# Feed-forward sums added straight from the banks and its loop written out, convolution taps dealt out, and a reordered second mixing layer

## The reference

```python
hn = rms_norm(h, g_mix_pre[i])
u = hn @ w_in[i]
q, k, v, xr, yg = jnp.split(u, [D_ATTN, 2 * D_ATTN, 3 * D_ATTN, 3 * D_ATTN + D_REC], axis=-1)
attn = neighborhood_attention(q, k, v, rpb[i])            # 8 heads of 128
rec = rglru_bidirectional(xr, conv_w[i], ...) * jax.nn.gelu(yg)   # 4-tap conv, two gates, two scans
mixed = jnp.concatenate([rms_norm(attn, g_attn_out[i]), rms_norm(rec, g_rec_out[i])], axis=-1) @ w_out[i]
h = h + rms_norm(mixed, g_mix_post[i])
fn = rms_norm(h, g_ffn_pre[i])
ff = (jax.nn.silu(fn @ w_ffn_gate[i]) * (fn @ w_ffn_up[i])) @ w_ffn_down[i]    # 5632 hidden
h = h + rms_norm(ff, g_ffn_post[i])
gate = jax.nn.sigmoid(rms_norm(h, g_ple_pre[i]) @ w_ple_gate[i])
h = h + rms_norm(gate * (p[i] @ w_ple_proj[i]), g_ple_post[i])
```

## Time and profile before

| | us |
|---|---|
| runs of the kernel | 4240.32, 4241.44, 4246.13 (median 4241.44) |
| the profiled execution | 4242.38 |
| its span in the profile | 4240.5 |
| PE busy | 4036.8 (95%) |
| DVE busy | 2759.2 (65%) |
| ACT busy | 1909.5 (45%) |
| POOL busy | 267.3 (6%) |
| mean granted share of PE's clock | 0.987 |

### The profile page before, as it was taken

One profiled execution on the slowest core, in us unless ns is written; L12 is line 12 of the kernel. 1 busy time (PEld: TensorE's weight loads), 2 busy tenths in 40 slices (PEclk: granted clock), 3 DMA queues, 4 the chain that ended last, 5 costly groups with the idle time before them and its releaser, 6 DMA issues.

```text
span 4240.5 us, 78225 instructions
## 1 busy us (share of the span) xinstructions
PE 4036.8 (95%) x30878; PEld 3846.5 (91%) x30878; DVE 2759.2 (65%) x3689; ACT 1909.5 (45%) x2772; POOL 267.3 (6%) x252
## 2 busy tenths in 40 slices
PE   2999999999999999999999999999888999999998
PEld 2999999999999999999999999999887888888888
DVE  7667777566678766677756576565466656565665
ACT  1443435334544344353533454454365544444465
POOL 0012121000000001212100000000000000000000
PEclk8999999999999999999999999999999999999999
DMA  9433333574358833333357434543443354555543
GB/s 392 154 130 118 132 115 128 206 272 154 140 191 315 298 136 123 120 133 119 130 192 278 160 138 149 182 176 133 168 146 114 137 189 179 179 179 185 179 143 120
DMA packets 114132, 724.38 MB, mean 171 GB/s; under 512 B 12608, under 2 KB 13056, under 8 KB 36224
## 3 DMA queue, kind: packets, MB, share of 16 engines
q1 hardware_dynamic: 88416, 639.17, 41.9%
q10 hardware_dynamic: 25504, 82.13, 5.4%
HBM read 719.09 MB, written 2.16 MB: 170 GB/s over the span
## 4 chain that ended last, share of the span: by engine, by line
PE 77%; DVE 8%; ACT 7%; issue 6%; DMA 1%; DVEq 0%; ACTq 0%; SPq 0%
PE bank L271 15%; PE bank L273 15%; PE bank L272 15%; PE bank L288 9%; PE bank L289 4%; ACT Wh L336 3%; PE bank L952 2%; PE bank L956 2%; PE bank L931 2%; DVE Wl L342 2%; DMA raw<-in_ada 1%; PE bank L2116 1%; PE bank L2118 1%; PE bank L2117 1%; PE bank L314 1%
## 5 line engine op out<-in xcount | busy, mean ns | idle before, releaser
L336 ACT CAST Wh<-raw 128x1024 fp32r<-128x1024 f32 x1140 | 1189.9, 1048 | 2020.8 <-PE bank L273 1509.8
L342 DVE TENSOR_TENSOR Wl<-raw,Wh 128x1024 fp32r<-128x1024 f32 x1140 | 1417.4, 1246 | 1002.0 <-ACT Wh L336 997.1
L271 PE MATMUL bank<-H,Wh 128*128 128x256 f32 x5536 | 1618.6, 292 | 0.5 <-ACT WS L1987 0.4
L272 PE MATMUL bank<-H,Wh 128*128 128x256 f32 x5536 | 1567.9, 283 | 0.0
L273 PE MATMUL bank<-H,Wl 128*128 128x256 f32 x5536 | 1567.2, 283 | 0.0
L271 PEld LDWEIGHTS bank<-H,Wh 128*128 128x128 f32 x5536 | 1063.0, 192 | 18.2 <-issue 17.4
L272 PEld LDWEIGHTS bank<-H,Wh 128*128 128x128 f32 x5536 | 1063.8, 192 | 9.2 <-issue 8.6
L273 PEld LDWEIGHTS bank<-H,Wl 128*128 128x128 f32 x5536 | 1062.2, 192 | 0.0
L288 PE MATMUL bank<-H,Wh 128*128 128x512 f32 x1600 | 561.9, 397 | 10.9 <-ACT WS L2170 5.6
L289 PE MATMUL bank<-H,Wl 128*128 128x256 f32 x1600 | 446.9, 279 | 0.0
L288 PEld LDWEIGHTS bank<-H,Wh 128*128 128x128 f32 x1600 | 300.3, 188 | 84.7 <-ACT WS L2170 6.2
(11 more groups left out here) (374 smaller groups left out, 4947.9 us busy)
## 6 DMA issues: line engine op xcount, KB each, us to landing
raw<-in_stream SPq DMA_DIRECT2D x572, 1024.0 KB, 4.8
WS<-in_ada ACTq DMA_DIRECT2D x94, 512.0 KB, 6.6
raw<-in_ada SPq DMA_DIRECT2D x32, 1024.0 KB, 7.5
gm_more<-in_ada ACTq DMA_DIRECT2D x20, 512.0 KB, 6.9
WS<-rows_d ACTq DMA_DIRECT2D x16, 512.0 KB, 4.8
KR<-in_ada ACTq DMA_DIRECT2D x14, 512.0 KB, 6.8
X<-in_x_t SPq DMA_DIRECT2D x1, 2048.0 KB, 17.4
WS<-in_rpb ACTq DMA_DIRECT2D x8, 256.0 KB, 2.9
```

What stands on the lines that cost most here:

```text
L271: pe.matmul(out[:, 0:T], wh, xh[:, kt, :], start=first, stop=False)
L272: pe.matmul(out[:, 0:T], wh, xl[:, kt, :], start=False, stop=False)
L336: act.copy(Wh[:, n % 4, :], raw[:, (sbk + 2) % 4, k * (D // 2):(k + 1) * (D // 2)]).then_inc(hi_ready, 1)
L342: dve.tensor_tensor(Wl[:, n % 4, :], raw[:, (sbk + 2) % 4, k * (D // 2):(k + 1) * (D // 2)], Wh[:, n % 4, :].bitcast(F32), ALU.subtract).t ...
```

## The change

It has two sets of edits.

The first: `dn` no longer copies its bank on ACT. DVE adds the bank to Y itself, ahead of its `dve_low` of the same half, and the three parts of `hidden` go behind the halves 0, 1 and 4. The feed-forward's loop of 5 rounds is a Python loop, so its instructions are written out. The delta rule's convolutions are dealt out, two taps behind each n from 2 to 13.

The second: neighborhood attention is one written-out run over 8 heads, whose ninth step projects the first three tiles of recurrence round 0 (so round 0 keeps tile 3 only); both groups of 7 spins go. The scores wait for k only, the transposes of v for v. The setup of the recurrence is split: DVE's part (`dve_rgset`) goes into the ninth step, ACT's table and functions behind round 0, `dve_lam` behind DVE's round 0. The eight attention squares get buffers of their own (`sq8`), follow tile 3 of round 0 on ACT, and are summed by PE behind tile 0 of round 1; the other sums move behind tile 3 of their round. In the chain, ACT's exponentials, tanh and table load go ahead of the casts of tile 2 and the square root between them; on DVE `gi` and its products go between the two subtractions of tile 2, and scans and `rec` ahead of those of tile 3. Eight spins are put behind the last sum.

```diff
-            def conv(m):
+            def conv(m, taps):
...
-                for t in range(4):
+                for t in taps:
...
-                if n in (4, 5, 7, 9, 11, 12):
-                    conv((4, 5, 7, 9, 11, 12).index(n))
+                if 2 <= n < 14:
+                    conv(n // 2 - 1, (0, 1) if n % 2 == 0 else (2, 3))
...
+        HN = D // 2 // P
-        def pe_na(pe, i):
+        def pe_na(pe):
...
-            for h in range(5):
+            for h in range(HN + 1):
                 x = (h - 1) % 2
                 if h:
-                    pe.wait_ge(tile_taken, i * 12 + (F2 + 3 * h + 2))
+                    pe.wait_ge(tile_taken, F2 + 3 * h - 1 + 2)
...
-                    if h < 4 and (h or n > 3):
+                    if h or n > 3:
...
                     if h and n == 1:
+                        pe.wait_ge(tile_taken, F2 + 3 * h + 2)
...
                     if h and n == 3:
-                        if h == 4:
-                            pe_spin(pe, 7)
...
+                        if h == HN and n == 1:
+                            S.wait(act, "pe", f"score{HN - 1}")
+                            st_rgset.wait(act, "dve", "z1")
...
+                        if h == HN:
+                            act.copy(rg_dst(b % 4), src).then_inc(tile_taken, 1)
...
+                        if h == HN:
+                            dve_rgset(dve)
...
+        def dve_lam(dve):
+            S = st_rgset
             S.wait(dve, "act", "ln")
             S.wait(dve, "dve", "pos")
             S.done(dve.tensor_tensor(lam4, lam4, SEC_X[:, 48:64], ALU.add), "dve", "softplus")
             S.wait(dve, "dve", "softplus")
             S.done(dve.tensor_scalar(lam4, lam4, -4.0, None, ALU.mult), "dve", "lam4")
+
+        def rg_dst(b):
+            return yin[:, b // 2, :] if b % 2 else xin[:, b // 2, 2:2 + T]
...
+        sq8 = [ws(4104 + j * T, T) for j in range(8)]
+
+        def rec_sq(j):
+            return sq8[j] if j < 8 else RSQ[:, j % 2, :]
...
             for b in range(4):
-                if gemm:
+                if gemm and (i or b == 3):
...
-                if i == 0:
-                    pe_rec_sum(pe, 2 * b)
-                    pe_rec_sum(pe, 2 * b + 1)
-                if i > 1 and b == 1:
-                    pe_rec_sum(pe, 2 * i + 4)
-                    pe_rec_sum(pe, 2 * i + 5)
+                if i == 1 and b == 0:
+                    for j in range(8):
+                        pe_rec_sum(pe, j)
...
+                if i > 1 and b == (3 if gemm else 1):
+                    pe_rec_sum(pe, 2 * i + 4)
+                    pe_rec_sum(pe, 2 * i + 5)
...
                 pe_rec_sum(pe, KT - 1)
+                pe_spin(pe, 8)
...
+                if chain and b == 2:
+                    S.wait(act, "dve", "log_a", r)
+                    S.done(act.activation(aa, ga_t, ACT.Exp), "act", "a")
+                    S.done(act.activation(hh, ga_t, ACT.Exp, scale=2.0), "act", "a2")
+                    S.wait(act, "act", "a2", r)
+                    S.done(act.activation(ga_t, ga_t, ACT.Tanh), "act", "tanh_la")
+                    act_table(act, ROOTS)
+                if gemm and (i or b == 3):
                     act_cast(act, i + Q_R, b, 0)
+                if chain and b == 2:
+                    S.wait(act, "dve", "expm1", r)
+                    S.done(act.activation(hh, hh, ACT.Sqrt, scale=-1.0), "act", "root")
+                if gemm and (i or b == 3):
                     act_cast(act, i + Q_R, b, 1)
...
+                if i == 0 and b == 3:
+                    for j in range(8):
+                        act_rec_square(act, j)
+                if i == 1 and b == 3:
+                    act_rstd(act, st_n[1], B[4][:, 0:T], 0, D // 2, "ra", "s7")
...
         def act_dn(act, q, f, run, par_, hidden):
-            S = st_dn
-            S.start("act")
             for b in range(4):
                 for k in range(2):
                     act_cast(act, q, b, k)
                     h = 2 * b + k
-                    if h < 2:
-                        S.wait_runs(act, "dve", run)
-                    else:
-                        S.wait(act, "dve", f"y{h - 2}", run)
-                    act.wait_ge(half_used, q * 8 + (h + 1))
-                    if h == 0:
-                        act.wait_ge(tile_taken, f + 2)
-                    act.copy(fd[k], G[k][:, :].rearrange("p (a b) -> p a b", b=T)).then_inc(tile_taken, 1)
...
         def dve_dn(dve, q, f, run, par_, hidden):
...
+                    h = 2 * b + k
+                    dve.wait_ge(half_used, q * 8 + (h + 1))
+                    dve.wait_ge(tile_taken, f + (h + 2))
+                    dve.tensor_tensor(Y[:, 2 * h:2 * h + 2, :], Y[:, 2 * h:2 * h + 2, :], G[k][:, :].rearrange("p (a b) -> p a b", b=T), ALU.add).then_inc(tile_taken, 1)
                     dve_low(dve, q, b, k)
-                    h = 2 * b + k
-                    dve.wait_ge(tile_taken, f + (h + 1 + 2))
-                    if h == 0:
-                        S.wait_runs(dve, "dve", run)
-                    S.done(dve.tensor_tensor(Y[:, 2 * h:2 * h + 2, :], Y[:, 2 * h:2 * h + 2, :], fd[k], ALU.add), "dve", f"y{h}")
+                    if hidden and h in (0, 1, 4):
+                        dve_hidden(dve, *hidden, parts=((0, 1, 4).index(h),))
...
-            with eng.Fori(0, (FF_GROUPS - 1) // 2) as i:
+            for i in range((FF_GROUPS - 1) // 2):
```

More of the change, by code:

```diff
@@ L1769, in pool_na, with dve_na @@
+        def pool_na(pool):
             S = st_na
             S.start("pool")
-            for h in range(4):
-                S.wait(pool, "dma", f"bias{h}", i)
+            for h in range(HN):
+                S.wait(pool, "dma", f"bias{h}")
                 v = bias[h % 2].rearrange("p a (r c) -> p (a r) c", c=64)
                 S.done(pool.tensor_tensor(v, v, const("near").unsqueeze(1).to_broadcast([P, 8, 64]), ALU.add), "pool", f"bias{h}")
-        def dve_na(dve, i):
+        def dve_na(dve):
@@ L1802, in dve_na @@
+                    if h < HN and n in (1, 4):
+                        at = 2 * h + n // 4
                         st_fin.wait(dve, "act", "r1")
@@ L1898, in pe_rec_sum @@
             S.wait(pe, "act", f"sq{j}")
-            S.done(pe.matmul(B[4][:, 0:T], ones, RSQ[:, j % 2, :], start=j in (0, 8), stop=j in (7, KT - 1)), "pe", f"s{j}")
+            S.done(pe.matmul(B[4][:, 0:T], ones, rec_sq(j), start=j in (0, 8), stop=j in (7, KT - 1)), "pe", f"s{j}")
         def pe_rg(pe, i, gemm, chain):
@@ L1965, in act_rg @@
                                                       bias=hb[:, bass.ds(r * 2 + (16 * x + 8 * z + m), 1)]), "act", f"gate{m}_{x}_{z}")
-                if chain and b == 2:
-                    S.wait(act, "dve", "log_a", r)
-                    S.done(act.activation(aa, ga_t, ACT.Exp), "act", "a")
-                    S.done(act.activation(hh, ga_t, ACT.Exp, scale=2.0), "act", "a2")
-                    S.wait(act, "act", "a2", r)
-                    S.done(act.activation(ga_t, ga_t, ACT.Tanh), "act", "tanh_la")
-                    act_table(act, ROOTS)
-                if chain and b == 3:
-                    S.wait(act, "dve", "expm1", r)
-                    S.done(act.activation(hh, hh, ACT.Sqrt, scale=-1.0), "act", "root")
-                if i == 0:
-                    act_rec_square(act, 2 * b)
-                    act_rec_square(act, 2 * b + 1)
                 if 1 < i < Q_RG and b == 0:
@@ L2011, in dve_rg @@
                     S.done(dve.tensor_tensor(gel, gel, yin, ALU.mult), "dve", "gel_arg")
-                if gemm:
+                if i == Q_RG and b == 2:
+                    for j in range(8):
+                        dve_lower(dve, st_n[1], mixed_w, j)
+                if chain and b == 2:
+                    S.wait(dve, "act", "tanh_la", r)
+                    S.done(dve.scalar_tensor_tensor(hh, hh, 1.0, ga_t, ALU.add, ALU.mult), "dve", "expm1")
+                if gemm and b == 2 and i:
+                    dve_low(dve, i + Q_R, b, 0)
+                if chain and b == 2:
+                    S.wait(dve, "act", "root", r)
+                    S.done(dve.scalar_tensor_tensor(gi_t, gi_t, 1.0, hh, ALU.add, ALU.mult), "dve", "gi")
+                    S.wait(dve, "dve", "gi", r)
+                    for m in range(2):
+                        S.done(dve.tensor_tensor(gi_t[:, 2 * m:2 * m + 2, :], gi_t[:, 2 * m:2 * m + 2, :], xc[:, m:m + 1, :].to_broadcast([P, 2, T]), ALU.mult), "dve", f"b{m}")
+                if gemm and b == 2 and i:
+                    dve_low(dve, i + Q_R, b, 1)
+                if chain and b == 3:
+                    for m in range(2):
+                        S.wait(dve, "dve", f"b{m}", r)
+                        S.done(dve.tensor_tensor_scan(hh[:, 2 * m, :], aa[:, 2 * m, :], gi_t[:, 2 * m, :], 0.0, ALU.mult, ALU.add), "dve", f"fwd{m}")
```

(9 more changed lines are left out.)

195 lines of the change are left out of this document (78 added, 117 removed).

## The result

The changed kernel takes 4180.27 us (median of four runs, 4177.27 to 4183.32), the kernel before beside it 4242.64. The ratio is 0.9848, with an interval from 0.9835 to 0.986: 62.4 us faster. The forecast was 4173, and 4180 lies in its range of 4161 to 4190; it lies 0.3 us outside the narrower 4165 to 4180, to which the prediction gave a chance of 0.71. Run once more beside another set of kernels, the changed kernel took 4185.39 against 4244.3, a ratio of 0.9855 (0.984 to 0.987), 58.9 us faster; single runs of it lie between 4177 and 4187, so a difference of 2 us between two kernels is small here.

The account below looks back on a forecast made before the run. PE was busy 95% of the span, so only its idle time, spins and half-speed stretches could be won. Terms summed to 68.7 us off 4242.4, giving 4173.7, and 4173 for the median; range 4161 to 4190.

Parts of the forecast that it names:

- Attention and round 0: Waits for the copy of v 13.8 us, two group ends 9.5, idle and slow time leaving round 0 12.4.
- Rounds 1 to 3: Recurrence: period 31.0 instead of 35.5 us, last chain starting at 99.7 instead of 109.1; 9.4 won, bounds 0 and 14.
- The feared wait for `Wl`: Recurrence rounds 2 and 3: line 271 waiting over 2 us for DVE's `Wl` would show the prediction wrong.
- Last pass: Recurrence's last pass, behind rounds 1 to 3: old order of ACT and DVE kept, so no gain forecast.
- Output projection's spins: Eight spins fill PE's 4.36 us idle ahead of line 310 and hold the clock: 2.7 us, bounds 0 and 3.4.
- Delta rule: Dealt-out taps remove line 911's 14 waits for DVE's subtraction: 4.1 us plus 0.2 for two first pairs, 4.3.
- Feed-forward: Loop pauses 8.1, entry 1.0, waits in `dn` 6.9 and end copy 0.6: 16.6 us, bounds 7 and 19.
- The additions: Feed-forward: DVE adding from the bank ends ten `dn` waits for ACT's copy, 6.9 us, and an end copy, 0.6.
- PE's pauses before line 288: Four later feed-forward rounds' starts: pauses read as the loop's jump, 8.1 us, gone when the loop is written out.
- the entry costs 1.0 more: Feed-forward loop's entry: 1.0 us more, taken as the loop's and gone with it.
- the prediction's own signs of being wrong: PE pauses in the written-out loop, a `Wl` wait over 2 us in rounds 2 and 3, or half clock there.
- Both rivals for a smaller gain: Recurrence gains nothing beyond round 0: 4185, chance 0.13; pauses at feed-forward rounds' starts not the loop's: 4182, chance 0.06.

Follow-up runs that it names:

- the second set's trace: The kernel before with the second set of edits alone, its feed-forward and loop unchanged: 4197.51 us against 4245.01, ratio 0.989.

## Why the prediction was right, and where it was not

- **Attention and round 0** (13.8 + 9.5 + 12.4 = 35.7): 35.9 in the trace. Waits priced with the modelled end and the slower first matmul (0.26 more than the table's idle time) came out right: from one head's scores to the next it takes 19.66 us instead of 21.40, 1.74 a head, where 13.8 for eight heads is 1.73.
- **Rounds 1 to 3** (9.4): 11.4. The period is 30.5, not 31.0, and the first convolution comes 6.3 behind round 0, not 6.7. The feared wait for `Wl` is there once, 1.6 us, not more, and the clock stayed up.
- **Last pass** (0): -2.9. "Behind that the last pass has the old order" was true of the order, not of the clock. The ple products behind the gates start 13.95 us behind the convolution in both kernels (3201.61 and 3144.69), and from there to the projection's first matmul of line 310 it takes 9.73 us instead of 6.82: the whole 2.9 is the products' half clock. In the kernel before the half clock had fallen on the gates' matmuls, ahead of that. The spins in the two pauses gave back 2.8 in the trace.
- **Output projection's spins** (2.7): 2.7, and 2.4 to 3.8 by the run without them.
- **Delta rule** (4.3): 7.4. The mechanism was right, the size was not: I left out the slower first matmul here, though I counted it at all other waits (0.29 + 0.10 + 0.04 for each wait instead of 0.29); layer 2 has another 0.08 a pair, and the two first pairs are worth 0.7, not 0.2.
- **Feed-forward** (16.6): 7.7. This is where the missing 9 us are, and it was two faults: the loop's price, and the interleaved start that came with it. The additions (6.9 for `dn`, 0.6 at the end) were right: `dn` 0.67 shorter ten times, and the end's wait 2.26 down to 0.46, 1.8 instead of 0.6. The failed step is "PE's pauses before line 288 ... with 0.16 + 0.1 each 8.1", "the entry costs 1.0 more", "both go with the loop". The pauses were the loop's and went; by the trace of the loop alone the feed-forward is 1.5 us shorter, not 9.1 (3.7 shorter than in the second set's trace, where the same old feed-forward takes 778.3; the medians give 3.2, and cannot tell it from nothing). Given back are the faster `gu` behind three edges (2.3, in part chance, as the second set's trace shows) and 0.22 in each of ten `dn` (2.2); a half-clock stretch in group 0, which the profile of before lacks and those of the changed kernel have too, takes 1.4; and the entry's 1.0 was never the loop's, since the step of 1.15 from matmul to matmul there is 1.12 without it. That leaves 0.7 of the 9.1 unassigned. The second fault: I read the loop's line and not what depends on its variable's type. The interleaved start in ten more groups took 4 to 7 us. Beside the additions the written-out `dn` is 0.79 shorter ten times (24.32 to 23.53), 1.0 more than forecast, so 16.6 - 7.6 + 1.2 + 1.0 - 3.9 = 7.3 of the 7.7 measured.
- The two edits of the feed-forward are not a sum of two terms. With the additions alone it takes 788.7 us, 12.6 more than before: the four jumps 1.9 more each, the `gu` behind them 11.2 more together (half clock, and the fast rhythm lost), a half clock of 1.4 in group 0, against 6.7 in `dn` and 1.8 at the end. With both, and group 0 alone interleaved, it takes 764.6. So writing the loop out was worth 1.5 by itself and 24 beside the additions, which alone would have been a loss. These are single traces, and the one of the additions alone is the slowest of its ten runs: by the medians that kernel loses 6.5 us, not 12, so 24 is a high figure.
- The rule of the Trainium skill (Runtime: NRT & Kernel Launch, section Instruction fetch mechanics), that a taken branch outside the fetched window stalls until the code is there, agrees with the packets: 16 KB of instructions 1.0 to 3.4 us behind the branch at the four taken edges of this loop, whose round has 1876 instructions in PE's records, and no such stop at the taken edges of the attention's and the delta rule's loops (1380 and 1210 instructions), where the branch lasts 0.2 us and PE has no pause. What the stall costs it does not say; here it was 2.1 and 3.9 us of PE.

Of the prediction's own signs of being wrong, one came in part: PE has pauses in the written-out feed-forward, 9.9 us idle of 732 where it forecast 0.14 us before each second half. Two are 2.4 us long, one in group 0, where the kernel before has it too, and one at the loop's entry, ahead of group 1's interleaved start. Of the 9.9, 9.3 are put down to VectorE's line 329, and none lies where the four jumps were. The other two did not come: the one wait for `Wl` is 1.6 us, below its 2, and rounds 1 to 3 ran at full clock.

Both rivals for a smaller gain fell by their own tests: the recurrence did gain beyond round 0, and the written-out code has no pause at the four later rounds' starts. The time of 4182 that the second of them gave came out all the same, by another mechanism. So the range held, and the 7 us between forecast and median are what is left of larger errors that cancel in part: +3.1 in the delta rule and +2.0 in rounds 1 to 3 stand against -2.9 in the last pass and -8.9 in the feed-forward, and the rest is within what one execution differs from the next.

## What to carry to other kernels

Price a loop's back edge together with what it meets: here the part of the weight block in flight that is left at the branch decided whether it cost 2 us or 4, so an edit elsewhere in the body can double it, and writing the loop out can be worth nothing or twenty us. When a hardware loop becomes a host loop, look for every test of the loop variable's type. A pause is worth more than its idle time by the modelled end and the slower first matmul, and one on the path of the end is worth its half clock too.

## What the runs showed that I had not expected

- An instruction fetch waits behind weights. At twelve edges it started within 0.25 us ahead of the end of the weight block in flight: 1.0 to 1.3 us behind the branch with a block issued 3.2 ahead of it, 3.1 to 3.4 with one issued 1.0 to 1.1 ahead, 2.9 to 3.0 with one issued 1.4 ahead.
- The same `gu` program runs in two steady rhythms, 45.23 and 44.4 to 44.5 us, at a granted clock of 1.00 in both. The faster one was seen behind a jump's pause, but not behind every one, and in the kernel with the addition behind the subtraction twice (44.38 and 44.39) behind a `dn` with no jump. What picks it stays open.
- Waits in written-out code were each 0.11 us longer than those in the loop (0.56 and 0.85 from matmul to matmul, against 0.41 and 0.70, less 0.03 in the matmul behind). Why stays open too.
- VectorE's addition of a 128x512 bank to Y took 685 ns, as much as the one that read `fd`.

```profile
L2195 DVE TENSOR_TENSOR Y<-Y,bank 128x512 f32<-128x512 f32 x88 | 60.3, 685 | 23.3 <-PE bank L2140 22.3
```
